# Second mixer: queries, decayed keys and transposed keys without zero halves, two heads side by side in the array's row halves

## The chip, the cores and the metric

The kernel runs on one core of a Trainium2 chip. The metric is the device time of one execution in microseconds; the median of a few runs counts. One further execution was profiled.

## The reference, cut to what matters

The whole computation is a block of two layers: a mixer with four kinds of attention and a feed-forward network, then a feed-forward network, a second mixer and another feed-forward network. It runs on 512 tokens of width 1024 in fp32. The change lies in the second mixer, in its gated linear attention with four heads, keys of 64 and values of 128 per head, and chunks of 64 tokens:

```python
def step(state, inp):                       # one chunk of 64 tokens
    qi, ki, vi, gi = inp
    bcum = jnp.cumsum(gi, axis=2)
    inter = jnp.einsum('bhck,bhkv->bhcv', qi * jnp.exp(bcum), state)
    diff = bcum[:, :, :, None, :] - bcum[:, :, None, :, :]
    decay = jnp.exp(jnp.where(causal, diff, -jnp.inf))
    scores = jnp.einsum('bhik,bhjk,bhijk->bhij', qi, ki, decay)
    out = inter + jnp.einsum('bhij,bhjv->bhiv', scores, vi)
    b_last = bcum[:, :, -1:, :]
    state = (state * jnp.exp(b_last[:, :, 0, :])[..., None]
             + jnp.einsum('bhck,bhcv->bhkv', ki * jnp.exp(b_last - bcum), vi))
    return state, out
...
o = o * lax.rsqrt(jnp.mean(o * o, axis=-1, keepdims=True) + EPS)
```

## The kernel before, in words

Every engine has a queue of instructions written out ahead (`Queue`, L20), with waits on other engines' semaphores in front of those that need them; each engine works its own queue strictly in that order. What stands where in the queues is decided by the generators of `mixer2` (L1330). `drive` (L438) steps them round robin: in each round it advances every generator to its next `yield`, in the order of the list at L1581: `proj`, two `rates`, two `keys`, `values`, two `states`, four `head`.

`proj` is the filler. It computes the projections as products of 24 matmuls each (8 blocks of 128 rows, 3 products of split halves), in two pieces of 12, one piece a round (`Stream.parts`, L358). Before a piece, `Stream.ahead` (L247) queues the split of a later weight piece into a rounded part (ScalarE, L263) and a rest (VectorE, L271); five pieces are kept ahead. After the second piece the product's bank is evicted by VectorE (`one`, L1354, an operation at L170); the projection alternates between two banks.

The 128 partitions hold the 64 keys of two heads, a pair j; there are two pairs. `keys(j)` makes on VectorE and ScalarE the decayed queries and keys. For the queries it keeps one tile per head, `QX[j][a]` and `QH[j][a]`, whose other 64 rows are zero (written by `clear`, L1407, with memsets on VectorE), so that a matmul over all 128 rows with the keys of both heads gives the scores of head a alone. The scores of a pair are 64 matmuls with 64 columns of weights and 16 moving columns, all into one bank; chunk c's results lie in column half c % 2. VectorE masks them into `PT[j]`. Then four transposes give `KT[j][a]`, where a is again the half of the rows that is not zero, and ScalarE copies them.

`values` transposes the values of each head into `VT[h]`. `states(j)` makes the seven state increments of both heads in two blocks, chunks 0 to 3 and 4 to 6, in two rounds, and VectorE chains them into `S[j]`. `head(h)` waits for the states and for the gates (`silu`), then one round (heads 0 and 2) or two rounds (heads 1 and 3), and queues 15 matmuls: state times `QH`, values times `PT`. VectorE scales the result, ScalarE squares it; a round later a matmul with ones sums the squares (L1572) and ScalarE takes Ln and Exp for the norm (`rstd_of`, L1671), each with its own load of the function table; a round after that VectorE multiplies (`Yt`).

Of the kernel before, what the change touches and what calls it, by code (L numbers as in the profile page):

```python
# [14 lines left out]
MUL, ADD, SUB, MAX, MIN = ALU.mult, ALU.add, ALU.subtract, ALU.max, ALU.min  # L15
# [1314 lines left out]
def mixer2(p, A, bank, W, pk, cA, col, hH, hL, rB, state, rstd_of, tap):  # L1330
    ident, ones = (cA[:, CPOS[n]:CPOS[n] + 128] for n in ("ident", "ones"))

    def run(xh, xl):
        ctx = ExitStack()
        tile = lambda w=T: p.sb(ctx, [128, w])
        m64 = tile(64)
# [58 lines left out]
        B = [tile() for _ in range(2)]  # L1395
        D = [tile() for _ in range(2)]
        E = [tile() for _ in range(2)]
        QX, QH = ([[tile() for _ in range(2)] for _ in range(2)] for _ in range(2))
        KH = k
        KX = [tile(2048) for _ in range(2)]  # L1400
        PT = [tile(1024) for _ in range(2)]
        KT = [[tile() for _ in range(2)] for _ in range(2)]
        VT = [tile(), v[0], v[1], v[2]]
        S = KX
        dec = tile(16)
# [1 line left out]
        def clear():  # L1407
            kz = [p.mset(t[:, :], 0.0, state.get("x_pe")) for t in KX]
            for j in range(2):
                for a in range(2):  # L1410
                    o = slice(64 - 64 * a, 128 - 64 * a)
                    for t in (QX, QH, KT):
                        zpad = p.mset(t[j][a][o, :], 0.0, state.get("x_pe"), q=p.dv)
                zpad = p.mset(PT[j][:, :], 0.0, state.get("x_pe"), q=p.dv)
            tok.update(kz=kz, zpad=zpad)

# [25 lines left out]
        def keys(j):  # L1442

            while Bt[j] is None or zt[3 + j] is None:
                yield
            kz, zpad = tok["kz"], tok["zpad"]
            kx = [None] * 4
            B3 = B[j][:, :].rearrange("p (c t) -> p c t", c=8)
            B4 = B[j][:, :].rearrange("p (c i t) -> p c i t", c=8, i=4)
            D4 = D[j][:, :].rearrange("p (c i t) -> p c i t", c=8, i=4)  # L1450
            k3 = k[j][:, :].rearrange("p (c t) -> p c t", c=8)
            KX4 = KX[j][:, :].rearrange("p (i c t) -> p i c t", i=4, c=8)

# [12 lines left out]
            e = yield from decay(0, B4, B4[:, :, :, 7:8].broadcast_to([128, 8, 4, 16]), True)  # L1466
            for a in range(2):
                r = slice(64 * a, 64 * a + 64)
                qx = efree[j] = p.stt(QX[j][a][r, :], q[j][r, :], 0.125, E[j][r, :], MUL, MUL, e, zt[1 + j])
            for i in range(4):  # L1470
                n = 16 * (i + 1)
                e = yield from decay(n, B3[:, :, 16 * i + 7:16 * i + 8].broadcast_to([128, 8, n]), B3[:, :, 0:n], True)
                kx[i] = efree[j] = p.tt(KX4[:, i, :, 0:n], k3[:, :, 0:n],
                                        E[j][:, 0:8 * n].rearrange("p (c t) -> p c t", c=8), MUL, e, zt[3 + j], kz[j])
            e = p.act(E[j][:, :], B[j][:, :], ACT.Exp, Bt[j], efree[j], scale=1.0 / 16)
            yield
            for a in range(2):
                r = slice(64 * a, 64 * a + 64)
                qh[j] = efree[j] = p.stt(QH[j][a][r, :], q[j][r, :], 0.125, E[j][r, :], MUL, MUL, e)
            e = yield from decay(64, B3[:, :, 63:64].broadcast_to([128, 8, 64]), B3, False)  # L1480
            kh = efree[j] = p.tt(KH[j][:, :], k[j][:, :], E[j][:, :], MUL, e)
            dc[j] = p.act(dec[:, 8 * j:8 * j + 8], B3[:, :, 63:64], ACT.Exp, scale=1.0 / 16)
            yield
            b = gb.next()
            o = b.t[:, :].rearrange("p (h m t) -> p h m t", h=2, m=4)
            for hh in range(2):
                QX4 = QX[j][hh][:, :].rearrange("p (c i t) -> p c i t", c=8, i=4)
                for c in range(8):
                    s = slice(64 * (c % 2), 64 * (c % 2) + 64)
                    for i in range(4):  # L1490
                        m = p.mm(o[s, hh, c // 2, 16 * i:16 * i + 16], KX4[:, i, c, :], QX4[:, c, i, :],
                                 True, True, b.free, qx, kx[3], kz[j], zpad, last=(hh == 1 and c == 7 and i == 3))
            for a in range(2):
                r = slice(64 * a, 64 * a + 64)
                b.free = ptt[j] = p.tt(PT[j][r, :].rearrange("p (c t) -> p c t", c=8)[:, :, 64 * a:64 * a + 64],
                                       b.t[r, :].rearrange("p (c t) -> p c t", c=8),
                                       m64[r, :].unsqueeze(1).broadcast_to([64, 8, 64]), MUL, m, small, zpad)
            yield
            b = gb.next()
            for n in range(4):  # L1500
                m = p.tr(b.t[:, 128 * n:128 * n + 128], KH[j][:, 128 * n:128 * n + 128], ident, kh, b.free,
                         last=n == 3)
            for a in range(2):
                r = slice(64 * a, 64 * a + 64)
                b.free = t = p.copy(KT[j][a][r, :], b.t[r, :], m)
            ktt[j] = t

        vtt = [None] * 4
        st = [[None] * 8 for _ in range(2)]
# [13 lines left out]
        def states(j):  # L1523
            while ktt[j] is None or vtt[2 * j + 1] is None:
                yield
            yield
            for c0 in (0, 4):
                b = gb.next()
                for c in range(c0, min(c0 + 4, 7)):
                    for hh in range(2):  # L1530
                        r = slice(64 * hh, 64 * hh + 64)
                        at = 128 * (c // 2)
                        m = p.mm(b.t[r, 128 * (c - c0):128 * (c - c0) + 128],
                                 KT[j][c % 2][:, at + 64 * hh:at + 64 * hh + 64], VT[2 * j + hh][:, at:at + 128],
                                 True, True, ktt[j], vtt[2 * j + hh], b.free,
                                 last=(hh == 1 and c == min(c0 + 4, 7) - 1))
                for c in range(c0, min(c0 + 4, 7)):
                    inc = b.t[:, 128 * (c - c0):128 * (c - c0) + 128]
                    new = S[j][:, 128 * (c + 1):128 * (c + 1) + 128]
                    if c == 0:  # L1540
                        st[j][1] = p.copy(new, inc, m, q=p.dv)
                    else:
                        st[j][c + 1] = p.stt(new, S[j][:, 128 * c:128 * c + 128],
                                             dec[:, 8 * j + c:8 * j + c + 1], inc, MUL, ADD, m, st[j][c], dc[j])
                    b.free = st[j][c + 1]
                yield

        ob = [None] * 4

        def head(h):  # L1550
            j, hh = h // 2, h % 2
            while st[j][7] is None or "silu" not in end:
                yield
            for _ in range(1 + hh):
                yield
            O, rs = (E[j], D[j]) if hh == 0 else (KT[j][0], KT[j][1])
            b = gb.next()
            for c in range(8):
                o = b.t[:, 64 * c:64 * c + 64]
                if c:  # L1560
                    p.mm(o, S[j][:, 128 * c:128 * c + 128], QH[j][hh][:, 64 * c:64 * c + 64], True, False,
                         st[j][c], qh[j], b.free)
                at = hh * 512 + 64 * c
                m = p.mm(o, VT[h][:, 128 * (c // 2):128 * (c // 2) + 128], PT[j][:, at:at + 64], c == 0, True,
                         ptt[j], vtt[h], b.free, last=c == 7)
            b.free = t = p.stt(O[:, :], b.t[:, :], col("gla_out_norm_2"), g[h][:, :], MUL, MUL, m, efree[j], st[j][7],
                               zt[9 + h])
            a = b.free = p.act(rs[:, :], b.t[:, :], ACT.Square, m, dfree[j], st[j][7], t)
# [7 lines left out]
            while "split" not in end:  # L1576
# [2 lines left out]

        clear()  # L1580
        drive([proj(), rates(0), rates(1), keys(0), keys(1), values(), states(0), states(1)] +  # L1581
              [head(h) for h in range(4)])
        p.tap_y("y2", Y, Yt)
        ctx.close()
        return hl
# [531 lines left out]
```

How the kernel before makes its waits and increments, by code:

```python
    def run(self, eng):  # L65
        for fn, sem, by in self.items:
            if fn is None:
                eng.wait_ge(sem, by)
            elif sem is None:
                fn(eng)
            else:
                fn(eng).then_inc(sem, by)
# [161 lines left out]
    def loads(self, sp, others):  # L234
        cut = np.cumsum([(nk + 3) // 4 for _, nk in self.units])
        for u, (src, nk) in enumerate(self.units):
            if u > 0:
                others(sp, u)
            if u >= RAW:
                for t in self.s_tail:
                    sp.wait_ge(t, int(cut[u - RAW]) // 2)
            sp.dma_start(self.raw[u % RAW][:, 0:nk * 128], src).then_inc(self.s_load[u % RAW], 16)
        for n in range(min(RAW, len(self.units))):
            sp.wait_ge(self.s_load[n], 16 * len(range(n, len(self.units), RAW)))
# [1394 lines left out]
        def load_x(sp, u):  # L1640
            for k in {1: range(1), 2: range(1, 8)}.get(u, ()):
                sp.dma_start(first[k][:, :], A["xt"][k * 128:(k + 1) * 128, :]).then_inc(ldx[k].sem, 16)
# [363 lines left out]
        def put_out(sp):  # L2006
            for n, cs, (sem, v) in early:
                sp.wait_ge(sem, v)
                store(sp, n, cs).then_inc(by_sp.sem, 16)
            sp.wait_ge(by_sp.sem, 16 * len(early))
```

## Time and profile before

| | |
|---|---|
| Median of 3 runs | 1695.58 us (1694.29 to 1701.33) |
| Profiled execution | 1688.55 us |
| Its span, first to last instruction | 1685.9 us |
| Mean granted TensorE clock | 0.993 |
| TensorE busy | 1651.4 us, 98% |
| VectorE busy | 821.7 us, 49% |
| ScalarE busy | 701.4 us, 42% |
| GpSimd busy | 256.8 us, 15% |

In the trace PE is the matmul side of TensorE and PEld its weight loads, DVE is VectorE, ACT ScalarE, POOL GpSimd. A form such as `128*64 128x16 f32` is a matmul with 128 active rows and 64 columns of weights, and 128 partitions by 16 moving columns. L198 is the helper `Prog.mm`, L206 `Prog.tr`, L170 `Prog.tt`, L158 `Prog.act`, L180 `Prog.stt`, L195 `Prog.mset`; a product's last matmul of a piece stands at L379. The second mixer lies at about 1105 to 1270 us of the span. Matmuls overlap, and their ends are modelled, so differences of starts say more than durations.

### The profile page before, as it was taken

Reading aid. Unit: us, or ns where it says so; the run is one execution under the profiler, and the core shown is the slowest. Engines: PE = TensorE matmul, PEld = TensorE weight load, DVE = VectorE, ACT = ScalarE, POOL = GpSimd, SP = SyncE. Lnnn points to the kernel's source line nnn. Section 1 sums busy time; section 2 is a strip of 40 time slices with the busy share of each in tenths; the row PEclk is TensorE's granted clock in tenths of the full one; section 3 lists DMA queues with packets and bytes.
Section 4 is the critical chain, followed back from the end, with each engine's and each line's share of the span. In section 5 each row is a group of like instructions: output and inputs, shape, how many; then the busy total and the mean of one; then the engine's idle time right before and its main releaser. Section 6 shows DMA issues by size and latency. Waiting matters only on the chain.

```text
span 1685.9 us, 21936 instructions
## 1 busy us (share of the span) xinstructions
PE 1651.4 (98%) x8672; PEld 1339.9 (79%) x8672; DVE 821.7 (49%) x1326; ACT 701.4 (42%) x1242; POOL 256.8 (15%) x216
## 2 busy tenths in 40 slices
PE   9999999999999999999999999999999999999997
PEld 6776777777888888868888888878887888888887
DVE  6576355466555542364444433377455444444333
ACT  6555455545444443354333333344533533333222
POOL 1221111001322210003222210000010022223000
PEclk9999999999999999999999999999999999999999
DMA  5220010323333233313322333322132332232332
GB/s 194 78 76 27 14 47 30 95 68 113 100 100 98 91 91 102 95 58 117 100 94 94 97 94 91 107 82 88 38 100 87 100 100 91 97 100 85 103 96 80
DMA packets 45285, 148.37 MB, mean 88 GB/s; under 512 B 5192, under 2 KB 8320, under 8 KB 45184
## 3 DMA queue, kind: packets, MB, share of 16 engines
q1 hardware_dynamic: 41760, 142.10, 26.1%
q10 hardware_dynamic: 3424, 4.89, 0.9%
q8 instruction: 68, 1.11, 0.3%
q14 instruction: 33, 0.27, 0.1%
HBM read 144.86 MB, written 2.10 MB: 87 GB/s over the span
## 4 chain that ended last, share of the span: by engine, by line
PE 91%; DVE 4%; ACT 3%; issue 1%; DMA 1%; POOL 0%; SPq 0%; DVEq 0%; ACTq 0%; POOLq 0%
PE bank L198 81%; PE bank L379 6%; DVE t L170 2%; PE bank L331 2%; ACT t L158 2%; PE bank L206 1%; DVE t L180 1%; ACT L158 1%; PE bank L307 1%; DMA t<-in_w_in 1%; ACT t L263 1%; DVE t L271 0%; DVE t L190 0%; DMA t<-in_w_out 0%; DVE t L176 0%
## 5 line engine op out<-in xcount | busy, mean ns | idle before, releaser
L198 PE MATMUL bank<-t 128*128 128x512 f32 (+8 forms) x7802 | 1553.4, 359 | 25.2 <-ACT t L158 6.7
L198 PEld LDWEIGHTS bank<-t 128*128 128x128 f32 (+4 forms) x7802 | 1192.3, 179 | 303.9 <-issue 35.1
L271 DVE TENSOR_TENSOR t<-t 128x512 fp32r<-128x512 f32 (+1 forms) x516 | 395.3, 790 | 607.0 <-ACT t L263 606.7
L263 ACT ACTIVATE t<-t 128x512 fp32r<-128x512 f32 (+1 forms) x540 | 321.6, 616 | 437.9 <-PE bank L379 352.9
L170 POOL TENSOR_TENSOR t<-t 128x512 f32<-128x512 f32 (+1 forms) x155 | 204.6, 1320 | 1160.6 <-ACT t L158 938.9
L158 ACT ACTIVATE t<-t 128x512 f32<-128x512 f32 (+6 forms) x345 | 198.9, 601 | 295.9 <-DVE t L170 142.4
L379 PE MATMUL bank<-t 128*128 128x512 f32 x498 | 193.7, 389 | 0.0
L170 DVE TENSOR_TENSOR t<-bank,t 128x512 f32<-128x512 f32 (+4 forms) x238 | 143.0, 628 | 57.1 <-PE bank L379 41.0
L180 DVE SCALAR_TENSOR_TENSOR t<-t 128x512 f32<-128x512 f32 (+4 forms) x158 | 103.8, 686 | 36.3 <-ACT t L158 33.9
L170 DVE TENSOR_TENSOR t<-t 128x512 f32<-128x512 f32 (+7 forms) x159 | 97.8, 636 | 46.6 <-ACT t L158 41.1
L379 PEld LDWEIGHTS bank<-t 128*128 128x128 f32 x498 | 93.5, 188 | 19.5
L165 ACT ACTIVATE t<-t 128x512 fp32r<-128x512 f32 (+3 forms) x81 | 48.3, 606 | 98.8 <-POOL t L170 96.8
L158 ACT ACT_TABLE_LOAD x51 | 65.4, 1283 | 6.7 <-issue 4.2
L180 DVE SCALAR_TENSOR_TENSOR t<-bank,t 128x512 f32<-128x512 f32 (+5 forms) x61 | 33.3, 562 | 69.2 <-PE bank L379 42.8
L165 ACT ACTIVATE t<-bank 128x128 f32<-128x128 f32 (+6 forms) x106 | 39.1, 388 | 65.6 <-PE bank L198 36.9
L271 POOL TENSOR_TENSOR t<-t 128x512 fp32r<-128x512 f32 x24 | 35.5, 1479 | 141.7 <-ACT t L263 141.5
L158 ACT ACTIVATE t<-bank,t 128x512 f32<-128x512 f32 (+5 forms) x67 | 38.1, 571 | 20.0 <-DVE t L176 12.3
L158 ACT ACTIVATE t<-bank 128x512 f32<-128x512 f32 x20 | 12.0, 598 | 54.1 <-PE bank L379 37.4
L206 PE MATMUL bank<-t 128*128 128x128 f32 x196 | 31.4, 291 | 1.6 <-DVE t L170 1.3
L331 PE MATMUL bank<-t 128*128 128x512 f32 x128 | 30.0, 389 | 0.0
L206 PEld LDWEIGHTS bank<-t 128*128 128x128 f32 x196 | 22.3, 145 | 7.6 <-issue 2.7
L331 PEld LDWEIGHTS bank<-t 128*128 128x128 f32 x128 | 24.0, 188 | 5.0
(24 smaller groups left out, 115.7 us busy)
## 6 DMA issues: line engine op xcount, KB each, us to landing
t<-in_ffn_w_up SPq DMA_DIRECT2D x88, 512.0 KB, 3.4
t<-in_w_in SPq DMA_DIRECT2D x50, 512.0 KB, 3.4
t<-in_ffn_w_down SPq DMA_DIRECT2D x48, 512.0 KB, 3.4
t<-in_ffn_w_gate SPq DMA_DIRECT2D x44, 512.0 KB, 3.4
t<-in_ffn_w_down SPq DMA_DIRECT2D x24, 384.0 KB, 3.1
t<-in_w_out SPq DMA_DIRECT2D x16, 512.0 KB, 3.4
t<-in_xt SPq DMA_DIRECT2D x8, 256.0 KB, 6.4
t<-in_xt ACTq DMA_DIRECT2D x8, 256.0 KB, 4.2
```

Of the source, the lines that this page charges most:

```text
L158: return self.av.do(lambda e: e.activation(out, in_, func, bias=bias, scale=scale, **({} if accum is None else {"accum_out": accum})), *de ...
L165: return q.do(lambda e: e.activation(out, in_, ACT.Copy), *deps, us=us)
L170: return q.do(lambda e: e.tensor_tensor(out, a, b, op), *deps, us=self.cost(out, q, True))
L180: return self.dv.do(lambda e: e.scalar_tensor_tensor(out=out, in0=a, scalar=s, in1=b, op0=op0, op1=op1), *deps, us=self.cost(out, self.dv, ...
L198: fn = lambda e: e.matmul(out, w, x, start=start, stop=stop, skip_group_check=True)
L206: fn = lambda e: e.transpose(out, in_, ident)
L263: self.p.av.put(lambda e: e.activation(hi, raw, ACT.Copy), self.s_head, 1, (self.s_load[u % RAW], 16 * (u // RAW + 1)), self.used(i - CUT) ...
L271: q.put(lambda e: e.tensor_tensor(lo, raw, hi.bitcast(F), SUB), self.s_tail[i % 2], 1, (self.s_head, i + 1), before, us=0.79 if q is self. ...
L307: fn = lambda e, o=outs[u], w=w, x=x, a=(k == 0 and n == 0), z=(k == 7 and n == 2): e.matmul(o, w, x, start=a, stop=z, skip_group_check=True)
L331: fn = lambda e, o=out, w=part(self.hi, u, k), x=xl[k][0], z=k == 7: e.matmul(o, w, x, start=False, stop=z, skip_group_check=True)
L379: pe.put(lambda e, lo=lo, x=x, stop=stop: e.matmul(out, lo, x, start=False, stop=stop, skip_group_check=True), self.used(i)[0], 1, us=0.227)
```

## The change

`QX`, `QH` and `KT` become one full tile per pair, with no zero rows; their memsets go, and each is written by one operation over 128 partitions. The scores, states and state times query matmuls take 64 rows, those of their own head (or their own chunk parity, for the states), and follow one another so that the row half alternates; each row half writes to its own bank. The states of a pair go into the queue as one block. A new generator `outputs(j)` queues the output matmuls of both heads of a pair together, chunk by chunk; `head` starts from its banks. `outputs(1)` stands in the list after `head(1)`.

```diff
-        QX, QH = ([[tile() for _ in range(2)] for _ in range(2)] for _ in range(2))
+        QX, QH, KT = ([tile() for _ in range(2)] for _ in range(3))
...
-                for a in range(2):
-                    o = slice(64 - 64 * a, 128 - 64 * a)
-                    for t in (QX, QH, KT):
-                        zpad = p.mset(t[j][a][o, :], 0.0, state.get("x_pe"), q=p.dv)
...
-            for a in range(2):
-                r = slice(64 * a, 64 * a + 64)
-                qx = efree[j] = p.stt(QX[j][a][r, :], q[j][r, :], 0.125, E[j][r, :], MUL, MUL, e, zt[1 + j])
+            qx = efree[j] = p.stt(QX[j][:, :], q[j][:, :], 0.125, E[j][:, :], MUL, MUL, e, zt[1 + j])
...
-            b = gb.next()
-            o = b.t[:, :].rearrange("p (h m t) -> p h m t", h=2, m=4)
-            for hh in range(2):
-                QX4 = QX[j][hh][:, :].rearrange("p (c i t) -> p c i t", c=8, i=4)
-                for c in range(8):
-                    s = slice(64 * (c % 2), 64 * (c % 2) + 64)
-                    for i in range(4):
-                        m = p.mm(o[s, hh, c // 2, 16 * i:16 * i + 16], KX4[:, i, c, :], QX4[:, c, i, :],
-                                 True, True, b.free, qx, kx[3], kz[j], zpad, last=(hh == 1 and c == 7 and i == 3))
+            two = [gb.next(), gb.next()]
+            QX4 = QX[j][:, :].rearrange("p (c i t) -> p c i t", c=8, i=4)
+            for c in range(8):
+                s = slice(64 * (c % 2), 64 * (c % 2) + 64)
+                at = 64 * (c // 2)
+                for i in range(4):
+                    for a, b in enumerate(two):
+                        r = slice(64 * a, 64 * a + 64)
+                        m = p.mm(b.t[s, at + 16 * i:at + 16 * i + 16], KX4[r, i, c, :], QX4[r, c, i, :],
+                                 True, True, b.free, qx, kx[3], kz[j], last=(a == 1 and c == 7 and i == 3))
             for a in range(2):
                 r = slice(64 * a, 64 * a + 64)
...
+                PT4 = PT[j][r, :].rearrange("p (h c t) -> p h c t", h=2, c=8)
+                for h, b in enumerate(two):
+                    b.free = ptt[j] = p.tt(PT4[:, h, a::2, :],
+                                           b.t[r, 0:256].rearrange("p (m t) -> p m t", m=4),
+                                           m64[r, :].unsqueeze(1).broadcast_to([64, 4, 64]), MUL, m, small, zpad)
...
-            for a in range(2):
-                r = slice(64 * a, 64 * a + 64)
-                b.free = t = p.copy(KT[j][a][r, :], b.t[r, :], m)
-            ktt[j] = t
+            b.free = ktt[j] = p.copy(KT[j][:, :], b.t[:, :], m)
...
+            two = [gb.next(), gb.next()]
             for c0 in (0, 4):
...
+                cs = range(c0, min(c0 + 4, 7))
+                for h in range(2):
+                    r = slice(64 * h, 64 * h + 64)
+                    for c in cs:
+                        a = slice(64 * (c % 2), 64 * (c % 2) + 64)
                         at = 128 * (c // 2)
...
+                        m = p.mm(two[c % 2].t[r, at:at + 128], KT[j][a, at + 64 * h:at + 64 * h + 64],
+                                 VT[2 * j + h][a, at:at + 128], True, True, ktt[j], vtt[2 * j + h],
+                                 two[c % 2].free, last=(h == 1 and c == cs[-1]))
+            for c in range(7):
...
+                if c == 3:
+                    yield
...
+        def outputs(j):
+            while st[j][7] is None or "silu" not in end:
+                yield
+            yield
+            two = [gb.next(), gb.next()]
+            for c in range(8):
+                if c:
+                    for a, b in enumerate(two):
+                        r = slice(64 * a, 64 * a + 64)
+                        p.mm(b.t[:, 64 * c:64 * c + 64], S[j][r, 128 * c:128 * c + 128], QH[j][r, 64 * c:64 * c + 64],
+                             True, False, st[j][c], qh[j], b.free)
+                for a, b in enumerate(two):
+                    at = a * 512 + 64 * c
+                    om[2 * j + a] = b, p.mm(b.t[:, 64 * c:64 * c + 64],
+                                            VT[2 * j + a][:, 128 * (c // 2):128 * (c // 2) + 128], PT[j][:, at:at + 64],
+                                            c == 0, True, ptt[j], vtt[2 * j + a], b.free, last=c == 7)
...
-            for _ in range(1 + hh):
-                yield
-            O, rs = (E[j], D[j]) if hh == 0 else (KT[j][0], KT[j][1])
...
+            while om[h] is None:
+                yield
+            O, rs = (E[j], D[j]) if hh == 0 else (QX[j], KT[j])
+            b, m = om[h]
...
-              [head(h) for h in range(4)])
+              [outputs(0), head(0), head(1), outputs(1), head(2), head(3)])
```

## Rows read from the trace of the kernel before

**Rows 1.** The page's busy times per engine, and the chain that ended last, by engine.

```profile
PE 1651.4 (98%) x8672; PEld 1339.9 (79%) x8672; DVE 821.7 (49%) x1326; ACT 701.4 (42%) x1242; POOL 256.8 (15%) x216
...
PE 91%; DVE 4%; ACT 3%; issue 1%; DMA 1%; POOL 0%; SPq 0%; DVEq 0%; ACTq 0%; POOLq 0%
```

**Rows 2.** Windows: stretch, busy us per engine (instructions), granted clock, DMA share, GB/s.

```profile
1170.00:1180.00 10.00, 10.00 (x263) 9.50 (x262) 4.20 (x8) 4.09 (x7) 0.00 (x0) 1.00 0.30 104
1200.00:1220.00 20.00, 20.00 (x123) 16.64 (x122) 7.36 (x10) 15.19 (x19) 1.56 (x1) 1.00 0.08 27
```

**Rows 3.** The chain that ended last, 1170 to 1221: start us, us, what.

```profile
1171.01 11.35 PE bank L198 x267
...
1183.46 2.51 PE bank L198 x11
1185.97 0.23 PE bank L379
1186.20 4.61 PE bank L198 x43
...
1191.04 4.22 PE bank L198 x35
...
1195.48 9.23 PE bank L198 x71
...
1216.12 4.25 PE bank L198 x15
```

**Rows 4.** Matmul groups by form, 1170 to 1217: busy us, mean ns, idle before.

```profile
L198 PE MATMUL bank<-t 128*64 128x16 f32 x256 | 8.7, 212 | 0.0
L198 PE MATMUL bank<-t 128*64 128x128 f32 x56 | 3.5, 276 | 0.0
```

**Rows 5.** TensorE's timeline in the first mixer: start us, us, line, form, count.

```profile
98.72 0.67 PE L198 MATMUL bank<-t 64*64 64x32 f32 x32
```

**Rows 6.** Matmul groups by form, 166.85 to 167.4.

```profile
L198 PE MATMUL bank<-t 64*64 64x64 f32 x16 | 0.7, 224 | 0.0
```

**Rows 7.** TensorE's timeline in windows of 0.01 us around 129.7 and 192.

```profile
129.63 0.38 PE L198 MATMUL bank<-t 64*128 64x128 f32 x2
...
130.06 0.50 PE L198 MATMUL bank<-t 128*128 128x512 f32 x1
...
191.72 0.49 PE L198 MATMUL bank<-t 128*128 128x128 f32 x2
...
192.13 0.28 PE L198 MATMUL bank<-t 128*64 128x64 f32 x2
```

**Rows 8.** ScalarE's timeline: the last of the four norm chains.

```profile
1220.10 1.28 ACT L158 ACT_TABLE_LOAD   x1
1221.39 0.69 ACT L158 ACTIVATE t<-bank,t 128x512 f32<-128x512 f32 x1
1222.10 1.28 ACT L158 ACT_TABLE_LOAD   x1
1223.39 0.63 ACT L158 ACTIVATE t<-t 128x512 f32<-128x512 f32 x1
```

**Rows 9.** VectorE's timeline: memsets, masks, and the work behind the outputs.

```profile
1097.85 1.57 DVE L195 MEMSET t<- 64x512 f32 x3 [0.16 <-issue]
...
1175.52 1.41 DVE L170 TENSOR_TENSOR t<-bank,t 64x512 f32<-64x512 f32 x2 [3.02 <-PE bank L198]
...
1215.56 0.69 DVE L271 TENSOR_TENSOR t<-t 128x512 fp32r<-128x512 f32 x1 [1.47 <-ACT t L263]
1216.16 0.68 DVE L170 TENSOR_TENSOR t<-bank,t 128x512 f32<-128x512 f32 x1
...
1218.21 2.39 DVE L170 TENSOR_TENSOR t<-t 128x512 f32<-128x512 f32 x2
```

**Rows 10.** TensorE's timeline: the transposes of the third head's values.

```profile
1145.34 0.66 PE L206 MATMUL bank<-t 128*128 128x128 f32 x4 [0.33 <-DVE t L170]
```

More of the change, by code:

```diff
@@ L1401, in run @@
         PT = [tile(1024) for _ in range(2)]
-        KT = [[tile() for _ in range(2)] for _ in range(2)]
         VT = [tile(), v[0], v[1], v[2]]
@@ L1476, in keys @@
             yield
-            for a in range(2):
-                r = slice(64 * a, 64 * a + 64)
-                qh[j] = efree[j] = p.stt(QH[j][a][r, :], q[j][r, :], 0.125, E[j][r, :], MUL, MUL, e)
+            qh[j] = efree[j] = p.stt(QH[j][:, :], q[j][:, :], 0.125, E[j][:, :], MUL, MUL, e)
             e = yield from decay(64, B3[:, :, 63:64].broadcast_to([128, 8, 64]), B3, False)
@@ L1483, in keys @@
             yield
-            b = gb.next()
-            o = b.t[:, :].rearrange("p (h m t) -> p h m t", h=2, m=4)
-            for hh in range(2):
-                QX4 = QX[j][hh][:, :].rearrange("p (c i t) -> p c i t", c=8, i=4)
-                for c in range(8):
-                    s = slice(64 * (c % 2), 64 * (c % 2) + 64)
-                    for i in range(4):
-                        m = p.mm(o[s, hh, c // 2, 16 * i:16 * i + 16], KX4[:, i, c, :], QX4[:, c, i, :],
-                                 True, True, b.free, qx, kx[3], kz[j], zpad, last=(hh == 1 and c == 7 and i == 3))
+            two = [gb.next(), gb.next()]
[8 more added lines that the diff above has]
+                                 True, True, b.free, qx, kx[3], kz[j], last=(a == 1 and c == 7 and i == 3))
             for a in range(2):
                 r = slice(64 * a, 64 * a + 64)
-                b.free = ptt[j] = p.tt(PT[j][r, :].rearrange("p (c t) -> p c t", c=8)[:, :, 64 * a:64 * a + 64],
-                                       b.t[r, :].rearrange("p (c t) -> p c t", c=8),
-                                       m64[r, :].unsqueeze(1).broadcast_to([64, 8, 64]), MUL, m, small, zpad)
+                PT4 = PT[j][r, :].rearrange("p (h c t) -> p h c t", h=2, c=8)
[3 more added lines that the diff above has]
+                                           m64[r, :].unsqueeze(1).broadcast_to([64, 4, 64]), MUL, m, small, zpad)
             yield
@@ L1502, in keys @@
                          last=n == 3)
-            for a in range(2):
-                r = slice(64 * a, 64 * a + 64)
-                b.free = t = p.copy(KT[j][a][r, :], b.t[r, :], m)
-            ktt[j] = t
+            b.free = ktt[j] = p.copy(KT[j][:, :], b.t[:, :], m)
         vtt = [None] * 4
@@ L1526, in states @@
             yield
+            two = [gb.next(), gb.next()]
             for c0 in (0, 4):
[L1528 to L1531, printed above, removed]
-                        at = 128 * (c // 2)
[L1533 to L1545, printed above, removed]
@@ L1546, in states @@
-                yield
-        ob = [None] * 4
+                cs = range(c0, min(c0 + 4, 7))
[3 more added lines that the diff above has]
+                        a = slice(64 * (c % 2), 64 * (c % 2) + 64)
+                        at = 128 * (c // 2)
+                        m = p.mm(two[c % 2].t[r, at:at + 128], KT[j][a, at + 64 * h:at + 64 * h + 64],
+                                 VT[2 * j + h][a, at:at + 128], True, True, ktt[j], vtt[2 * j + h],
+                                 two[c % 2].free, last=(h == 1 and c == cs[-1]))
@@ new lines, in states @@
+            for c in range(7):
+                inc = two[c % 2].t[:, 128 * (c // 2):128 * (c // 2) + 128]
+                new = S[j][:, 128 * (c + 1):128 * (c + 1) + 128]
+                if c == 0:
+                    st[j][1] = p.copy(new, inc, m, q=p.dv)
+                else:
+                    st[j][c + 1] = p.stt(new, S[j][:, 128 * c:128 * c + 128],
+                                         dec[:, 8 * j + c:8 * j + c + 1], inc, MUL, ADD, m, st[j][c], dc[j])
+                two[c % 2].free = st[j][c + 1]
+                if c == 3:
+                    yield
@@ new lines, in run @@
+        ob = [None] * 4
+        def outputs(j):
+            while st[j][7] is None or "silu" not in end:
+                yield
+            yield
[11 more added lines that the diff above has]
+                                            c == 0, True, ptt[j], vtt[2 * j + a], b.free, last=c == 7)
@@ L1550, in head @@
+        om = [None] * 4
         def head(h):
             j, hh = h // 2, h % 2
-            while st[j][7] is None or "silu" not in end:
+            while om[h] is None:
                 yield
-            for _ in range(1 + hh):
-                yield
-            O, rs = (E[j], D[j]) if hh == 0 else (KT[j][0], KT[j][1])
[L1557 to L1565, printed above, removed]
+            O, rs = (E[j], D[j]) if hh == 0 else (QX[j], KT[j])
+            b, m = om[h]
```

## Prediction, made before the change was run

> **What bounds the kernel now.** I read the page's busy times and chain first. TensorE is busy 98% of the span and 91% of the chain that ended last is its work [rows 1], so a microsecond taken off TensorE's queue is a microsecond off the end, unless it comes back as a wait. Then the windows over the second mixer: TensorE is full in every stretch touched, at the full clock (1.00, the 2.4 GHz level), while ScalarE alone comes near its limit, 15.19 of 20 us, where the heads' norms are [rows 2]. Then the chain through that stretch [rows 3]: the reader sees pieces of 12 product matmuls (11 at L198, one at L379; 2.51 + 0.23, call it 2.72 us) and between them the mixer's own blocks. One round of `drive` puts one piece and one block into the queue. A "record" below is one matmul row of the trace; each fp32 matmul leaves two. Net of the 11 product matmuls (2.49) the blocks take: scores 11.35 - 2.49 = 8.86 for 256 records; states 4.61 - 2.49 = 2.12 for 32 and 4.22 - 2.49 = 1.73 for 24; outputs of two heads 9.23 - 2.49 = 6.74 for 60, and the other two heads the same; four records of the norm sums 4.25 - 2.49 = 1.76, so 0.88 per head.
>
> **Scores.** The count stays (128 matmuls, 256 records); only 64 rows are active in each, and the two heads alternate row halves. Now they take 8.7 us [rows 4], 34 ns each, with eight records in one column half, then eight in the other. Bounds: with all four quarters of the array in turn the first mixer's 64x64 form does 32 records from 98.72, each 0.22 long, in 0.67: (0.67 - 0.22)/31 = 14.5 ns; with only two quarters in turn, (0.7 - 0.22)/15 = about 31 ns [rows 5, 6]. That is 3.7 to 7.9 us. I take half of today's 34 ns, 17 ns and 4.35 us: each row half does in parallel what the whole did, in the same runs of eight. Saved 4.5 (1.0 to 5.1).
>
> The Trainium skill (TensorE: Matmul & The Clock Gate, section "Wait - 56ns, not 53.3ns?") says that start-to-start never drops below about 25 ns however small the moving side is. By it, as an estimate, the scores would take 256 x 25 = 6.4 us and save 2.5. The 14.5 ns of [rows 5] are below that floor, though for bursts of 32 only.
>
> **States.** 56 records of 128x64 by 128 columns take 3.5 us busy [rows 4]; less 0.27 of latency for each of the two blocks, 53 ns each with two column halves at once, and the rest of the 3.85 us, 0.44 per block, is entering and leaving. After: four quarters; the busiest has 8 records per pair, so 16 rounds of 106 ns = 1.70 plus one entry, since both pairs' steps go in as one block: 2.14. Saved 1.7; if only two quarters overlap, 0.4.
>
> **Outputs.** Here the saving is eaten. The state product (28 matmuls, 56 records) goes to 64 rows and both heads overlap, but score times values stays at 128 rows, and the new order alternates them: two of the one, two of the other, at each chunk. Steady, a full-array record costs 6.74/60 = 0.112, so a chunk of both heads 8 x 0.112 = 0.89. A change of shape is not free: two 64x128 rounds between full-array neighbours last from 129.63 to 130.06, 0.43 against 0.22 for two unbroken ones; two full-array records between 128x64 neighbours from 191.72 to 192.13, 0.41 [rows 7]. So each change costs about 0.2. With 64 moving columns instead of 128 the last one streams some 0.05 less: state group 0.37, value group 4 x 0.112 + 0.19 - 0.05 = 0.59, sum 0.96, that is 0.07 more than now. Fourteen such chunks (seven per pair): 0.95 us lost. Bounds: 3.1 gained if the change were free (14 x 0.22), 2.3 lost if each were 0.05 dearer (28 x 0.05 more).
>
> The Trainium skill (TensorEngine Tiling (Array Packing), section "Key Properties") has the rule: changing the tiling mode, not just the tile, drains the TensorE. It speaks against this order; the trace agrees, with the 0.2 us above. It gives no price.
>
> **Order of the blocks.** This is the largest term. Before, heads 0 and 2 put in their outputs in one round (A), heads 1 and 3 in the next, so ScalarE had two norm chains, a product's split, then two more. After, `outputs(0)` and `outputs(1)` both go in in round A and all four heads' sums and norms in round A+1. One norm chain is two table loads, Ln and Exp: 1220.10 to 1224.02, or 3.95 from load to load [rows 8]. ScalarE's queue then holds: split of round A+1, four chains, split of round A+2. From the first head's sum on: 0.69 + 1.28 + 0.63 = 2.6, 3 x 3.95 = 11.85, split 0.6, and on VectorE, which is in order, the tail of that split 0.6 and only behind it the eviction of the product that ended in round A+2, 0.6 with its latency 0.1 (1215.56 and 1216.16 in [rows 9]): 16.4 us. TensorE meanwhile has three more sums (2.64) and the pieces of rounds A+2, A+3, A+4 (8.16): 10.8. Round A+5 begins a product in that same bank (the projection has two, each product two pieces). It waits 16.4 - 10.8 = 5.6 us. Before, the eviction at 1216.16 was 7 us ahead of its use. Behind it VectorE still has two convolution steps, four products Yt (1218.21: 1.2 each for two), two tails and an eviction [rows 9] and the other bank is wanted two pieces later: 0.2 to 1.4 more, I take 0.7. Bounds of both: 0, if the chains run elsewhere in the queue than I read, to 9. With TensorE at 98% there is hardly any idle time later that could take it back.
>
> **Off the path.** VectorE loses 12 memsets of 64x512 (four rows of three, 1.57 each [rows 9]: 6.3 us), but TensorE is busy throughout there; nothing. Four products over 64 partitions fewer, some 0.7 each; before them TensorE waits once for an eviction, 0.33 at 1145.34 [rows 10], which can go: 0.3 gained. The masks become 8 of 64x256 instead of 4 of 64x512 (1.41 for two [rows 9]); priced between 0.3 and 0.7 each they take 2.4 to 5.6 against 2.8. They now free the banks of the states, but two pieces and the transposes (6.3 us) lie between; if that cover went, up to 2. KT's copy is one of 128x512 instead of two of 64x512: ScalarE saves 1.2, hidden. The state steps on VectorE (14, about 0.35) now run behind the last matmul of their pair, 5 us plus two tails, against 5.4 of pieces and the first outputs, which need no late state: no wait. The banks handed out change, and each is free rounds before its use.
>
> **Sum.** -4.5 - 1.7 + 0.95 - 0.3 + 5.6 + 0.7 = +0.75, say +0.8 on the profiled execution: span 1685.9 to 1686.7, its time 1688.55 to 1689.35. The median of the runs is 1695.58, 0.4% above that execution; the same step gives 1696.4.
>
> **The rivals.**
> - *No stall.* The norm chains cost TensorE nothing, for example because the scheduler's rounds fall otherwise and two product pieces lie more between. For it: the chain rows show TensorE unbroken through the same eight table loads now. Against: 16.4 against 10.8 is not close. Then 0.75 - 6.3 = -5.55: 1690.0.
> - *Slower.* A floor on the rate of records, in place of the work in them: the queue cannot feed four quarters through 256 records in a row (the fast rows are a burst of 32). If the scores stay at 34 ns a record, the 4.5 are gone and the stall, which counts only from the outputs on, stays: 0.75 + 4.5 = +5.25, 1700.8; at the 31 ns of two quarters +4.3. Above 17 ns a record the gains no longer pay the stall. The Trainium skill's floor of 25 ns (the page and section above) would be a mild form of it, by estimate +2.8 and 1698.4.
> - *Free changes of shape.* Outputs gain 3.1 instead of losing 0.95, the rest as forecast: 0.75 - 4.05 = -3.3, 1692.3. The 0.2 us rows are against it.
> - *The change does not do what it says* (row halves run one after the other): scores as now, outputs another 14 x 0.22 = 3.1 worse: 0.75 + 4.5 + 3.1 = +8.3, 1703.9. The first mixer's 14.5 ns speak against it.
>
> **How the numbers follow.** Forecast 0.60, no stall 0.14, slower 0.13, free changes 0.08, the last 0.05. The forecast's own range, from the terms' bounds, is 1692 to 1700. All but the last stay within 0.5% (8.5 us, about what a measurement of this kernel tells from none, its three runs being 7 apart), so "within" holds most: 0.82; faster 0.10 from "no stall" with scores at 14.5 ns and a low draw; slower 0.08 from the last case and a stall at its upper bound. The range 1689 to 1702 takes in all but the last and the far ends.
>
> **What would show it.** In the changed profile: the 64x64 group of 16 columns near 4.4 us; the states one block near 2.1; the outputs' block about 14.3 for both pairs, with starts 0.2 apart at each change of shape; eight table loads in a row on ScalarE with no split between; then TensorE idle some 5.6 us behind VectorE's eviction, three pieces after the norm sums. No such gap, or one of another place, makes the prediction wrong in its largest term, whatever the total says.

## Result and profile after

| | before | after |
|---|---|---|
| Median of 15 runs | 1695.28 us (1683.99 to 1701.33) | 1710.24 us (1701.55 to 1716.20) |
| Ratio to before, 95% interval | | 1.0093 [1.0074, 1.0111] |
| Span of the profiled execution | 1685.9 us | 1713.0 us |
| Mean granted TensorE clock | 0.993 | 0.976 |
| TensorE busy | 1651.4 us | 1671.9 us |

The change made the kernel 0.93% slower, about 15 us; 1696.4 was forecast, with 1702 as the upper end. The page of the profile after, first its busy times as in [rows 1], then its line PEclk: the granted TensorE clock in 40 equal slices of the span, in tenths of full speed.

```profile
PE 1671.9 (98%) x8672; PEld 1352.4 (79%) x8672; DVE 813.4 (47%) x1314; ACT 700.1 (41%) x1240; POOL 256.6 (15%) x216
...
PEclk9999889999999999999999999999799999999999
```

TensorE has as many records as before and is busy 20 us longer. The PEclk line has dips: one in the fifth and sixth slices, where the first mixer is, and one near three quarters of the span, where the second is. The chain that ended last shows the blocks there (start us, us, what; against [rows 3]):

```profile
1181.28 3.50 PE bank L198 x194
1184.78 1.66 issue
1186.44 7.17 PE bank L198 x72
...
1194.78 2.51 PE bank L198 x11
1197.29 0.23 PE bank L379
1197.51 4.67 PE bank L198 x64
...
1205.12 25.53 PE bank L198 x131
```

And the windows (columns as in [rows 2]) show at which clock each ran:

```profile
1181.20:1184.80 3.60, 3.58 (x195) 3.48 (x194) 1.70 (x4) 1.64 (x3) 0.00 (x0) 1.00 0.43 150
1186.40:1193.40 7.00, 6.96 (x73) 5.87 (x74) 2.21 (x5) 0.00 (x0) 0.00 (x0) 0.53 0.01 2
1197.40:1204.90 7.50, 7.50 (x81) 6.37 (x81) 6.38 (x17) 0.63 (x1) 0.00 (x0) 1.00 0.18 72
1205.00:1210.60 5.60, 5.60 (x50) 4.79 (x48) 0.69 (x1) 0.00 (x0) 1.09 (x1) 1.00 0.30 95
1210.60:1231.20 20.60, 20.60 (x87) 17.56 (x86) 3.51 (x5) 4.19 (x6) 0.00 (x0) 0.50 0.00 1
1231.20:1242.80 11.60, 11.60 (x44) 7.91 (x43) 0.00 (x0) 10.56 (x12) 0.00 (x0) 1.00 0.00 0
1242.80:1248.50 5.70, 0.02 (x1) 0.00 (x0) 1.41 (x3) 5.66 (x8) 0.00 (x0) 0.68 0.00 1
1248.50:1252.60 4.10, 4.07 (x12) 3.27 (x13) 4.07 (x5) 1.37 (x3) 1.60 (x1) 0.62 0.38 128
```

The seventh number is the granted clock: 1.00 is the 2.4 GHz level, 0.50 the 1.2 GHz level. There are three falls: behind a stop in the scores, inside the outputs' block, and in the gap behind the norms. Before the gap TensorE's timeline reads:

```profile
1242.43 0.39 PE L379 MATMUL bank<-t 128*128 128x512 f32 x1
1248.53 4.20 PE L198 MATMUL bank<-t 128*128 128x512 f32 x11 [5.71 <-DVE t L170]
```

ScalarE's timeline up to its end, the last of four norm chains and the split behind them, and VectorE's, where the eviction stands behind the tail of that split (answering to [rows 8, 9]):

```profile
1242.62 1.28 ACT L158 ACT_TABLE_LOAD   x1
1243.91 0.69 ACT L158 ACTIVATE t<-bank,t 128x512 f32<-128x512 f32 x1
1244.62 1.28 ACT L158 ACT_TABLE_LOAD   x1
1245.91 0.63 ACT L158 ACTIVATE t<-t 128x512 f32<-128x512 f32 x1
1246.45 0.61 ACT L263 ACTIVATE t<-t 128x512 fp32r<-128x512 f32 x1
```

```profile
1247.09 0.69 DVE L271 TENSOR_TENSOR t<-t 128x512 fp32r<-128x512 f32 x1 [18.28 <-ACT t L263]
1247.70 0.68 DVE L170 TENSOR_TENSOR t<-bank,t 128x512 f32<-128x512 f32 x1
```

Where the time of the second mixer went, from these rows and [rows 3]:

| stretch | before | after | difference | forecast |
|---|---|---|---|---|
| scores and one piece | 11.35 | 3.50 + 1.66 + 7.17 = 12.33 | +1.0 | -4.5 |
| states, without pieces | 3.85 | 4.67 - 2.49 = 2.18 | -1.7 | -1.7 |
| four outputs and one piece | 13.48 + 2.49 = 15.97 | 25.53 | +9.6 | +0.95 |
| gap | 0 | 5.71 | +5.7 | +5.6 |
| piece behind the gap | 2.66 | 4.20 | +1.5 | 0 |

That is +16.1, near the 15 of the medians. The two profiled executions are 27.1 apart. Of the rest 10.3 lie ahead of the scores (they start at 1171.01 before and at 1181.28 after), in the first mixer, whose instructions are the same. The windows of before and of after there show why: the clock differs, and with it how much was done in the 30 us.

```profile
200.00:230.00 30.00, 30.00 (x188) 22.20 (x185) 15.11 (x39) 16.50 (x35) 3.43 (x4) 1.00 0.08 25
```

```profile
200.00:230.00 30.00, 30.00 (x146) 21.75 (x145) 10.63 (x29) 10.95 (x26) 2.18 (x3) 0.66 0.02 6
```

Of the 13 executions profiled in this study ten have a stretch of 10 to 21 us at 0.50 between 200 and 225 us. Before, outputs_full_rows and three_right have none: these profiles are lucky ones, and before's stands 7 us under its median.

### The profile page after: what moved, and what is told of

The parts are those of the page before. It is cut to its first block, busy times and chain, and to the rows that moved or that the text cites. A ratio compares the mean times of both kernels' runs of the same rounds, so it can differ in the third digit from the quotient of the medians.

```text
span 1713.0 us, 21924 instructions
## 1 busy us (share of the span) xinstructions
PE 1671.9 (98%) x8672; PEld 1352.4 (79%) x8672; DVE 813.4 (47%) x1314; ACT 700.1 (41%) x1240; POOL 256.6 (15%) x216
## 4 chain that ended last, share of the span: by engine, by line
PE 90%; DVE 4%; ACT 4%; issue 1%; DMA 1%; POOL 0%; SPq 0%; DVEq 0%; ACTq 0%; POOLq 0%
PE bank L198 81%; PE bank L379 6%; DVE t L170 2%; ACT t L158 2%; PE bank L331 2%; PE bank L206 1%; ACT L158 1%; DVE t L180 1%; PE bank L307 1%; DMA t<-in_w_in 1%; ACT t L263 1%; DVE t L271 0%; DVE t L190 0%; DMA t<-in_w_out 0%; DVE t L184 0%
## 5 line engine op out<-in xcount | busy, mean ns | idle before, releaser
L198 PE MATMUL bank<-t 128*128 128x512 f32 (+10 forms) x7802 | 1573.6, 363 | 32.2 <-DVE t L170 12.0
L198 PEld LDWEIGHTS bank<-t 128*128 128x128 f32 (+4 forms) x7802 | 1204.4, 182 | 318.9 <-issue 44.8
L180 DVE SCALAR_TENSOR_TENSOR t<-t 128x512 f32<-128x512 f32 (+3 forms) x154 | 101.0, 686 | 36.1 <-ACT t L158 33.8
L165 ACT ACTIVATE t<-bank 128x128 f32<-128x128 f32 (+5 forms) x104 | 37.7, 384 | 78.1 <-PE bank L198 47.3
```

The costliest lines, as they stand in the source:

```text
L165: return q.do(lambda e: e.activation(out, in_, ACT.Copy), *deps, us=us)
L180: return self.dv.do(lambda e: e.scalar_tensor_tensor(out=out, in0=a, scalar=s, in1=b, op0=op0, op1=op1), *deps, us=self.cost(out, self.dv, ...
L198: fn = lambda e: e.matmul(out, w, x, start=start, stop=stop, skip_group_check=True)
```

## Experiments

Ratios are to the kernel before, timed on the same chip between the others.

| kernel | ratio | 95% interval | runs | granted clock of a run: median (highest) |
|---|---|---|---|---|
| before | | | 84 | 0.989 (0.996) |
| after, the change | 1.0093 | [1.0074, 1.0111] | 15 | 0.980 (0.986) |
| outputs_apart | 1.0022 | [1.0001, 1.0044] | 12 | 0.984 (0.989) |
| by_shape | 1.0024 | [1.0001, 1.0048] | 12 | 0.986 (0.991) |
| scores_apart | 1.0075 | [1.0050, 1.0099] | 8 | 0.982 (0.986) |
| three_together | 0.9953 | [0.9929, 0.9976] | 12 | 0.988 (0.997) |
| three_right | 0.9927 | [0.9895, 0.9959] | 7 | 0.993 (0.997) |
| outputs_full_rows | 1.0031 | [1.0011, 1.0051] | 12 | 0.984 (0.993) |
| scores_alone | 0.9995 | [0.9970, 1.0020] | 12 | 0.987 (0.994) |
| states_alone | 0.9992 | [0.9971, 1.0013] | 12 | 0.990 (0.992) |
| four_heads_at_once | 1.0081 | [1.0052, 1.0109] | 6 | 0.985 (0.986) |
| scores_alone_apart | 0.9976 | [0.9953, 0.9999] | 12 | 0.989 (0.994) |
| row_halves_in_series | 1.0030 | [1.0003, 1.0057] | 12 | 0.986 (0.990) |

The last column is the mean over the whole span. The falls of the change are not those of one profile only: its median is 0.009 lower, about 15 us of clock over 1700 us, and the three falls of its profile come to 17 (half of 7.0, 20.6 and 6.9 us).

**The theory**: each of the three falls of the clock follows from what a block does, and the falls, with the forecast gap, are the loss. **The rival**: the clock falls by chance, as in the first mixer, and only waits count. Each experiment is one edit; its expectation stands ahead of its result.

### The order of the blocks

```diff
             while st[j][7] is None or "silu" not in end:
                 yield
-            yield
+            for _ in range(1 + j):
+                yield
```

> The changed kernel, with outputs(1) one round later, so that two norm chains, a split of weights and two more chains follow one another as before. Read so far: in the changed kernel's trace TensorE idles 5.71 us behind VectorE's eviction at 1248.5 and then does a piece in 4.20 instead of 2.66 us at a granted clock of 0.62; its outputs' block takes 25.69 us for 131 records at 0.50 from 1215 on; the scores stop for 1.66 us and go on at 0.53. Theory (the clock falls are a consequence of what this mixer's blocks do, each its own): the gap and the slow piece behind it go, 5.7 + 1.5 = 7.2 us, the other two falls stay: 1710.2 - 7.2 = 1703.0. Rival 1 (the clock falls by chance from run to run, as it does in the first mixer, and only waits count): 5.7 us, 1704.5; no fall need stand anywhere. Rival 2 (the gap only moves, to another eviction or split): 1710.

Ratio 1.0022, 12 us less than the change's 1.0093. Its trace has no gap of 5.7 us and no half clock in its place; the outputs still run partly at 0.50. The two blocks, and behind them the same two in the kernel before:

```profile
1202.23 12.91 PE L198 MATMUL bank<-t 128*128 128x64 f32 x71
...
1215.21 15.89 PE L198 MATMUL bank<-t 128*128 128x512 f32 x75
```

```profile
1195.32 9.39 PE L198 MATMUL bank<-t 128*128 128x64 f32 x71
...
1204.78 11.12 PE L198 MATMUL bank<-t 128*128 128x512 f32 x75
```

Each is a pair's outputs with 11 product matmuls (the second with the sums of two heads too). The gain is 5 us more than expected; the outputs run 17 us at half clock in place of 20.6, which explains 1.7. The rest stays open; it is within the two intervals.

The same order alone, on the kernel before:

```diff
-            for _ in range(1 + hh):
+            for _ in range(1):
                 yield
```

> The kernel before in every matmul, with one thing moved: heads 1 and 3 queue their outputs in the same round as heads 0 and 2, so that four norm chains stand in a row in ScalarE's queue, as in the changed kernel. Theory (the order alone makes the gap, as the prediction worked it out, and a gap of 5.7 us lets the clock fall, for another 1.5): TensorE idle 5.7 us behind VectorE's eviction three pieces after the norm sums, 0.9 more at most at the next bank, half clock behind it: +7.2 to 8, ratio 1.0045. Rival (the gap needs the shorter blocks ahead of it, since ScalarE's chains start at the same place in both): no gap or under 3 us, ratio under 1.002.

```profile
1235.61 0.39 PE L379 MATMUL bank<-t 128*128 128x512 f32 x1
1241.72 4.97 PE L198 MATMUL bank<-t 128*128 128x512 f32 x11 [5.73 <-DVE t L170]
```

The gap is there to 0.1 us, with no new shape in the kernel: the order of the queues makes it. The piece behind takes 4.97, so gap and fall cost 8.0. The ratio says 14 us, interval 9 to 18, from six runs only. In the profile the clock fell in two more places: from 1290.8 to 1294.3, and in the scores, which have here the kernel before's own shapes and order. The chain that ended last, and the window behind it:

```profile
1180.14 6.55 PE bank L198 x194
1186.69 0.21 issue
1186.90 7.85 PE bank L198 x73
```

```profile
1188.40:1195.30 6.90, 6.90 (x38) 5.61 (x35) 2.07 (x3) 0.00 (x0) 0.00 (x0) 0.51 0.00 0
```

Scores and piece take 14.61 in place of 11.35. Nothing in this kernel's edit stands ahead of them, and the profiles of before and of states_alone, with the same scores, have no fall there. So chance, the rival, has a part in this place too; 3.3 for it and some 1.7 for the fall at 1290.8 (half of 3.5) bring the 8.0 to 13.

### The outputs: change of shape or not

```diff
-            for c in range(8):
-                if c:
-                    for a, b in enumerate(two):
-                        ...
+            for c in range(1, 8):
+                for a, b in enumerate(two):
+                    ...                        # state times queries, 64 rows
+            for c in range(8):
                 for a, b in enumerate(two):
                     ...                        # values times scores, 128 rows
```

In this kernel and in three_together a part of the state's product is left out of the sums, as the flags that start an accumulation were kept and do not fit the new order; three_right has them right. Instructions and shapes are all there.

> The changed kernel, with the output matmuls of a pair grouped by shape: first the 14 of state times queries (64 rows, both heads in turn), then the 16 of values times scores (128 rows), so 2 changes of shape per pair in place of 14. Theory (the changes of shape leave the array idle often enough that the clock falls): the block stays at 1.00; its own 14 x 0.37 and so on shrink by 12 pairs of changes of about 0.3 us, 3.6 us, and the half clock's 9 us go: 1710.2 - 12.6 = 1697.6. Rival (the clock falls there for another reason, such as the 64 moving columns or chance): only the changes of shape, 3.6 us, 1706.6, and the block still at 0.50 in part.

```profile
1200.18 13.51 PE L198 MATMUL bank<-t 64*128 64x64 f32 x131
1213.52 0.39 PE L379 MATMUL bank<-t 128*128 128x512 f32 x1
```

13.51 in place of 25.69 in the changed kernel's timeline, for the same 120 records and a piece, at 1.00: 11.7 us by the ratio, 12.6 expected. The counter-test keeps 64 moving columns, order, gap and scores of the change, and gives the state product its 128 rows back, against queries with zero halves as before:

```diff
-                        r = slice(64 * a, 64 * a + 64)
-                        p.mm(b.t[:, 64 * c:64 * c + 64], S[j][r, 128 * c:128 * c + 128], QH[j][r, 64 * c:64 * c + 64],
+                        p.mm(b.t[:, 64 * c:64 * c + 64], S[j][:, 128 * c:128 * c + 128], QH[j][a][:, 64 * c:64 * c + 64],
```

> The changed kernel in everything (same queue order, stall and scores), but the state times query matmuls of the outputs take all 128 rows again, against queries padded with zeros: no change of shape inside the block, same count and same 64 moving columns. Theory (the changes of shape are what let the clock fall in the outputs): block of 120 records in 13.4 us at 1.00, in place of about 23; the stop in the scores, the gap of 5.7 and their half-clock stretches stay: 11.7 us less than the changed kernel as in by_shape, ratio to before about 1.002 to 1.003. Rival (the clock falls there because the scores' stop came shortly before it, or because 120 small matmuls stand in one block): half clock again in the block, ratio near 1.008.

```profile
1187.40:1203.30 15.90, 15.90 (x132) 15.45 (x131) 3.52 (x5) 2.84 (x5) 1.09 (x1) 1.00 0.10 34
```

The block is at 1.00 from end to end, and the ratio is 1.0031, inside the 1.002 to 1.003 expected. The scores' fall comes as far ahead of the outputs as in the change (from 1169.5 to 1176.4) and does not bring one there. So it is the alternation of shapes, 28 changes in a row, that leaves TensorE at half clock: the two other kernels that alternate, outputs_apart and scores_apart, have the fall, the four that do not, with either way of doing without, have none.

The Trainium skill (TensorE: Matmul & The Clock Gate, "What's actually happening") says that a clock gate sets the rate by how busy the engine has recently been. By the profile's busy time the trace does not bear this out, since TensorE counts as busy for 20.60 of the 20.60 us that lost the clock. About 0.4 of each chunk's 0.96 us goes into its two changes of shape; that the clock is taken down for these 0.4 is not shown by any run.

### The scores: stop and fall

```diff
+            if j:
+                yield
             two = [gb.next(), gb.next()]
             QX4 = QX[j][:, :].rearrange("p (c i t) -> p c i t", c=8, i=4)
...
-            yield
+            if not j:
+                yield
             b = gb.next()
```

> The changed kernel, with the scores of pair 1 one round after those of pair 0, a product piece of 12 matmuls between them; its transposes stay where they were. Theory (the burst of 256 records at 17 ns empties the instructions fetched ahead; the stop of 1.66 us is a fetch, and the clock falls behind it): no stop, no fall, scores two blocks of 2.2 us: 1.7 + 3.5 = 5.2 us less, 1705.0. Rival 1 (the stop is a fetch, the fall has to do with the 64x64 form's small work and comes all the same): 1708.5. Rival 2 (the stop has nothing to do with the burst's length): as the changed kernel, 1710.2, with a stop in one of the blocks.

1.0075: 3 us less than the change, 5.2 expected. No stop is left in its trace and no half clock near the scores; the outputs and the gap have theirs as in the change. On the kernel before, first the new scores as one burst, then apart:

> The kernel before, with the new scores alone (queries of both heads in one tile, row halves in turn, two banks, eight masks); states and outputs as before. Theory: the burst at 17 ns a record stops after about 190 records for 1.4 to 1.9 us, the clock is at half for 6.8 us behind it, which costs 3.4: -4.5 + 1.7 + 3.4 = +0.6 us against before, ratio 1.000. Rival 1 (a stop, but no fall without the later blocks): -2.8, 0.998. Rival 2 (the faster scores reach only after the outputs' clock is cured, so something later waits instead): over 1.002.

> The kernel before with the new scores alone and those of pair 1 one round after those of pair 0. Theory: two bursts of 128 records of 2.2 us each, no stop, no half clock behind them: 4.4 us less than before, ratio 0.9974. Rival (a short burst lets the clock fall too, or waits appear where pair 1's masks come a round later): 1.000 and a granted clock under 1 near the scores.

0.9995 and 0.9976, the second 4.1 us under before (4.4 expected), with an interval that just leaves out 1. Its two blocks of 128 records, the whole stretch at the full clock:

```profile
1178.40:1187.00 8.60, 8.60 (x276) 7.83 (x276) 3.98 (x9) 4.35 (x8) 0.00 (x0) 1.00 0.27 97
```

The stop in one burst is most likely a wait for instructions: it stands behind the 194th record in all five kernels that had the new scores in one burst at 17 to 18 ns, "issue" says that TensorE waited for nothing that the profile shows, and in blocks of half the length there is no stop. The changed kernel's DMA view has a single instruction packet between 1183.6 and 1185.2 and none from there to 1186.4; TensorE starts again at 1186.44, 2.8 us behind the packet. No row ties the two together.

```profile
q8 instruction: 1, 0.02, 5.2%
```

But is it the stop that lets the clock fall? In scores_alone it was only 0.6 us long, and 6.9 us of half clock followed all the same. So the same matmuls with less overlap, to take away the stop (the edit as against scores_alone):

```diff
-            for c in range(8):
-                ...
-                for i in range(4):
-                    for a, b in enumerate(two):
+            for a, b in enumerate(two):
+                for c in range(8):
+                    ...
+                    for i in range(4):
```

> The new scores on the kernel before, with one change of order: all 128 records of head a's row half, then those of the other, so that only two quarters of the array work at a time. Same shapes, same instructions, no change of tile shape. Theory 1 (the clock falls because the burst is stopped for instructions): at about 31 ns a record, 8 us in all, the fetch keeps up, no stop and no fall: -1.0 us against before, 0.9994. Theory 2 (the clock falls because 64x64 matmuls of 16 columns are too little work for the array, stop or no stop): no stop, yet half clock in or behind the block, 3.4 us: +2.4, 1.0014.

```profile
1179.40:1184.80 5.40, 5.40 (x163) 5.37 (x163) 2.36 (x6) 3.20 (x6) 0.00 (x0) 1.00 0.44 157
1184.80:1195.20 10.40, 10.40 (x111) 9.34 (x109) 2.96 (x7) 0.00 (x0) 0.00 (x0) 0.51 0.01 2
```

No stop, and the clock falls inside the block; ratio 1.0030. My first reading, that the stop brings the fall, is refuted: a long block of these small matmuls has the fall without it. Whether the stop adds to it in the burst is open. Two short blocks with other work between are spared.

### The states

```diff
-            for c0 in (0, 4):
-                b = gb.next()
-                ...
+            two = [gb.next(), gb.next()]
+            for c0 in (0, 4):
+                ...                            # as in the change, one block, four quarters
```

> The kernel before, with the new states alone (transposed keys of both halves in one tile, four quarters of the array, one block for a pair's seven chunks, one copy by ScalarE). Theory: 3.85 us of two blocks become 2.1 in one, nothing waits: -1.7 us, ratio 0.999, no half clock in the mixer. Rival (the four-quarter block lets the clock fall as the outputs' does, or VectorE's state steps, all behind the last matmul of a pair, make the outputs wait): ratio 1.001 or more, with idle time before the outputs or a granted clock under 1.

0.9992, 1.4 us below before against 1.7 expected, smaller than the interval, so the times show no gain; no half clock between 1160 and 1270. The size rests on the traces (3.85 to 2.18 in the change).

### All three

> All three edits: outputs(1) a round later, outputs grouped by shape, scores of pair 1 a round later. Theory of the clock as consequence: 1710.2 - 7.2 - 12.6 - 5.2 = 1685, that is 10 us below the kernel before, of which 4.5 scores, 1.7 states, 3 outputs. Rival (clock by chance, only waits and changes of shape count): 1710.2 - 5.7 - 3.6 - 1.7 = 1699.2.

> The three edits together (outputs(1) a round later, outputs grouped by shape, pair 1's scores a round later), with the accumulation flags mended: only the first matmul into each output bank starts an accumulation, all others add or, where nothing was written, overwrite. The instructions are the same in number, order and shape as in three_together, which ran at 0.9953 of before, so the theory (the flags cost no time) gives the same 0.995, about 8 us below before, with no gap and no half clock between 1170 and 1260. Rival (starting or not starting an accumulation changes the pace of the 64-column matmuls): a block of outputs longer than its 12 to 13 us and the gain gone.

The edit as against three_together:

```diff
-                         True, False, st[j][c], qh[j], b.free)
+                         c == 1, False, st[j][c], qh[j], b.free)
...
-                                            c == 0, True, ptt[j], vtt[2 * j + a], b.free, last=c == 7)
+                                            False, True, ptt[j], vtt[2 * j + a], b.free, last=c == 7)
```

0.9953 and 0.9927, both clear of 1. By the rival's sum three_together was to come out above the kernel before (1699.2); it is 8 us below. The second, which computes everything, is by its ratio 12 us faster than the kernel before and 28 faster than the change. The 12 has luck in it: the median clock of its seven runs is 0.993, where the 84 of before have 0.989 and three_together, the same instructions, 0.988. Profile against profile, both of them lucky ones, it is 1677.8 against 1685.9, the 8 us of three_together. Its outputs by pair, 8.07 and 9.90 against 9.39 and 11.12 in the kernel before:

```profile
1189.62 8.07 PE L198 MATMUL bank<-t 64*128 64x64 f32 x71
...
1197.75 9.90 PE L198 MATMUL bank<-t 128*128 128x512 f32 x75
```

```profile
1100.00:1300.00 200.00, 195.65 (x1207) 159.43 (x1206) 114.28 (x188) 86.62 (x138) 12.36 (x9) 1.00 0.24 80
```

The granted clock is 1.00 over the whole mixer. The two kernels differ in flags alone; their intervals overlap.

Over all 13 profiles the falls of the second mixer stand so:

| block | profiles with a fall in or behind it |
|---|---|
| new scores in one block | 6 of 6 |
| new scores in two blocks | 0 of 4 |
| scores as before | 1 of 3 (four_heads_at_once) |
| outputs with alternating shapes | 3 of 3 |
| other outputs | 0 of 10 |
| gap of 5.7 us | 5 of 5 |

Four profiles (by_shape, four_heads_at_once, outputs_apart, scores_apart) have a further fall of 3.5 to 4 us between 1280 and 1296, the others not, with the same instructions there. The theory holds for the three places of the change; the rival holds for this late one and for the old scores.

## Why the prediction was wrong

- **Scores**: 17 ns a record, 4.35 us in all. 194 records came in 3.50 us, 18 ns each: right, and below the 25 ns of the Trainium skill's floor (TensorE: Matmul & The Clock Gate, "Wait - 56ns, not 53.3ns?"), now for 194 records in a row. Wrong in the rest: the stop (the "slower" rival had the queue failing to feed the array, though as a rate), and the clock. Scores with their piece changed by +1.0 in place of -4.5.
- **States**: 2.14 forecast, 2.18 measured.
- **Outputs**: at the full clock a chunk was to take 0.96. State groups start at 1205.44 and 1206.40, 0.96 apart, in the timeline of the changed kernel:

```profile
1205.44 0.44 PE L198 MATMUL bank<-t 64*128 64x64 f32 x4
...
1206.40 0.44 PE L198 MATMUL bank<-t 64*128 64x64 f32 x4
```

  So the price of a change of shape was right to 0.01 us, at the full clock. From 1210.6 on the block ran at 0.50, and +9.6 stands where +0.95 was forecast.
- **Order of the blocks**: a gap of 5.6 behind VectorE's eviction, three pieces after the norm sums: 5.71, in that place, and shown by the order alone on the kernel before. The sum behind it was right too: from the end of the first head's sum (1232.06) to the end of the eviction (1248.38) it is 16.3 where 16.4 stood, and TensorE's work in that time, to 1242.82, is 10.8. The 0.7 behind it did not come. The 1.5 of the slow piece was not in the sum.
- **The step that failed** is the one that was never priced. The text read "TensorE is full in every stretch touched, at the full clock (1.00, the 2.4 GHz level)" off the kernel before and carried 1.00 over to blocks whose shape, pace and waits it was about to change. The three falls cost, from the windows: the outputs some 8.6 (9.6 less 0.95), the scores about 3.5, the gap 1.5, in all 13.6; with the stop, 1.7, that is 15.3, and less the 0.7 that did not come 14.6. The distance between forecast and result is 14 to 15 (+0.8 and +15). The trace of before held a warning: among the first mixer's small matmuls the clock was at half several times, as here for 16 records of the form 64x64, behind a wait of 1.4 us:

  ```profile
  141.78:142.60 0.82, 0.82 (x16) 0.82 (x16) 0.00 (x0) 0.82 (x4) 0.00 (x0) 0.50 0.00 0
  ```

- **No rival** had it. "Free changes of shape" and "no stall" were rightly held unlikely. The terms of the sum nearly cancelled, which made the forecast look safer than its parts.

## What to carry to other kernels

Where TensorE is the bound, price its clock with the same care as its matmuls: a long block of small tiles or of alternating shapes can lose to the slower level what its new shape gains or more (the scores gained 4.5 us and lost 3.5 to the clock and 1.7 to the stop, the outputs gained nothing and lost 8.6), and a wait of 5.7 us cost another 1.5 to 2.3 behind it. Group matmuls by the tile shape they use, keep bursts of tiny ones short, with full-size work between, and read the granted clock stretch by stretch. Two generators that move into the same round bring all their followers into one queue; what stands behind those in the queue, on every engine, belongs to the price.

## What the runs showed that was not expected

- TensorE was counted busy 100% of stretches in which the clock was taken down (20.60 of 20.60 at 0.50): busy time is no guard against it.
- A burst of 256 records (512 instructions with the weight loads) at 17 to 18 ns stops behind the 194th record for 0.4 to 1.9 us, in all five kernels that had it. At 31 ns a record it does not stop. At 34 ns, the pace of before, two profiles have no stop and one (four_heads_at_once) has 0.2 us, again behind the 194th.
- The same instructions in the first mixer ran at 1.00 in one execution and at 0.66 over 30 us in another; a single profile can be luckier than the median of its kernel by 7 us (before) and by 13 (outputs_full_rows).
